# Moving the context chunk's two final states of a bidirectional scan from the mixer stage to the norm behind the output projection

## The chip, the cores and the metric

One core of one Trainium2 chip runs the whole program. The metric is the device time of one execution in microseconds, as a median of several runs. The engines are PE (TensorE matmul; PEld is its weight load), DVE (VectorE), ACT (ScalarE), POOL (GpSimd) and SP (SyncE, which here only issues transfers). Each runs its own instructions in order, and semaphores order them among each other.

## The reference

The kernel is one inference step of a trunk of two layers (model width 1024) over 256 latent tokens and 128 context tokens. Each layer has three token mixers side by side (pooling, differential attention, a bidirectional Mamba-2 scan), a gated merge, an output projection, and a gated FFN with a small convolution. What the change touches is the scan:

```python
def ssd_chunked_scan(x, dt, a, bm, cm, h0):
    ...
    xdt = (x.astype(jnp.float32) * dt[..., None]).reshape(b, nc, q, h, pdim)
    ...
    decay_to_end = jnp.exp(a_cs[..., -1:] - a_cs)
    chunk_states = jnp.einsum('bclhn,bhcl,bclhp->bchpn', bc, decay_to_end, xdt)
    chunk_decay = jnp.exp(a_cs[..., -1])

    def step(state, inp):
        st, dec = inp
        return state * dec[..., None, None] + st, state

    h_final, h_enter = lax.scan(step, h0.astype(jnp.float32), ...)
    ...
    y_off = jnp.einsum('bclhn,bchpn,bhcl->bclhp', cc, h_enter, jnp.exp(a_cs))
    return (y_diag + y_off).reshape(b, n, h, pdim), h_final
```

A chunk has 128 tokens. The 256 latent tokens are chunks 0 and 1, the context is chunk 2. Latent scans start from a given state, so each direction needs one chunk state to enter the other latent chunk. The context scan starts from zero and has a single chunk, so its two chunk states (forward and backward) enter nothing: they are the final states `new_state_ssd`, an output of each layer.

## The kernel before

Every weight tile of 128x128 is split into a high part `wh` and a low part `wl` (ACT rounds, DVE subtracts), and every activation tile likewise (`hh` and `hl`, `mh` and `ml`, `ah` and `al`). A product of the projections is three matmuls (lines 976 to 978). The program is a fixed list of 140 units a layer, each one block of weights of 512 KB at most: XBC 8, U 4, Q 4, K 4, V 4, Z 4, GATE 24, BRANCH 12, OUT 8, UP 44, DOWN 24. Each engine's program is a loop over this list. In unit u ACT and DVE also prepare the weights of unit u + 3, in three buffers (`ahead`; lines 1336 and 1747). All orders are written out by hand in the four engine programs.

From the first Z unit on (MIX0 = unit 24) each unit is also a slot s = u - MIX0 of the mixers. At the end of each slot PE runs a piece of attention or scan between two units, and ACT and DVE have the matching pieces. What matters here:

- Slots 14 to 16, `chunk`: the scan's inputs are transposed into `xt` and `bg`, one chunk each.
- Slots 17 to 20, `chunk_state` (PE, line 1202): one task of `S_TASKS` each, (chunk, direction). DVE weights `xt` into the single buffer `xw` one slot earlier (`weighted`, line 2033), PE makes two fp32 products of 256 columns into `mix7`. Tasks 0 and 1 are the latent ones, and DVE turns them into entering states `hst` (`enter_state`). Tasks 2 and 3 are the context's. ACT copies them from `mix7` into `th` and `cv` (line 1611), and POOL sends these to HBM (line 788).
- Slots 18 and 19: the attention norm. ACT makes the reciprocal roots `rst` (lines 1602 and 1603), DVE applies them to `ot` (line 2124), behind `weighted` of slot 19 and the small `exponents` in its queue.
- From slot 19 on, every second slot, one of six scan tasks y: PE spreads decays over the partitions (`rows`, line 1218), DVE makes exponents (`decays`, line 2058), ACT takes their exp (lines 1621 and 1623), DVE finishes the matrices `ee` (`matrices`, lines 2068 to 2072), and two slots after its `rows` PE reads out (`scan_out`, line 1246). DVE gates the result (`gate_z`, lines 2084 and 2088), which for the first task waits until the state transfers have read `cv`.
- Slot 27 is the last GATE unit; behind it the pooling result `ut` is split into `hh` and `hl` (line 1752), and its memory is free. BRANCH follows (BRANCH0 = unit 52), then OUT (unit 64).

At the norm behind OUT, ahead of the first UP unit (UP0 = unit 72), PE sums squares (`mean_squares`), ACT takes the inverse root and makes the first `hh` (line 1452). Meanwhile PE runs `fill_gap`: three products of 384 columns that nobody reads (line 844). Then `joint` runs the first three UP units tile by tile (line 1075). In UP, ACT reads each bank into `cv` (`evac`, line 1499), DVE adds the convolution's side taps (line 1928), and after each odd unit ACT and DVE split the gated product into `ah` and `al` (lines 1361 and 1752). The tile of index 14 of `al` begins where `ut` lay.

Of the kernel before, what the change touches and what calls it, by code (L numbers as in the profile page):

```python
# [30 lines left out]
P = 128  # L31
# [11 lines left out]
NCH = 3  # L43
# [185 lines left out]
S_TASKS = ((0, 0), (1, 1), (2, 0), (2, 1))  # L229
# [91 lines left out]
def build(nc, wstream, whead, par, bias, tab, xs, xp, cvec, cvec_rows, kc, vc, st0, fng, y, newk, newv, news):  # L321
    ctx = ExitStack()
    with ctx:
# [34 lines left out]
        with ExitStack() as a:  # L358

            head = sb("head", [P, MOD_HEAD, P * KT], where=a)  # L360
# [86 lines left out]
        end_state = [b[:, :, :].rearrange("p a t -> p (a t)")[:, 0:4 * P] for b in (th, cv)]  # L447
# [114 lines left out]
        st_done = sem("st_done")  # L562
        bc_done = sem("bc_done")
# [118 lines left out]
        def _(pool):  # L682
# [68 lines left out]

            pool.wait_ge(head_done, KT // 2)
            pool.dma_start(fg[:, :], fng).then_inc(fg_in, 16)
            for l in range(DEPTH):
# [6 lines left out]
                for u in range(NU):  # L761
                    if u == OUT0:

                        pool.wait_ge(mod_used, sum(lu < (l, OUT0) for lu in MODS))
                        pool.wait_ge(st_out, 32 * (l + 1))
                        pool.wait_ge(gb_done, count(l, 24, 23))
                        pool.dma_start(crow[:, :, :], cvec_rows).then_inc(crow_in, 16)
# [17 lines left out]
                    if u in (MIX0 + SLOT_S + 2, MIX0 + SLOT_S + 3):  # L785
                        k = u - MIX0 - SLOT_S - 2
                        pool.wait_ge(st_done, count(l, 4, 2 + k))
                        pool.dma_start(news[l, k], end_state[k]).then_inc(st_out, 16)
# [34 lines left out]
        def _(pe):  # L823
# [370 lines left out]
            def chunk_state(l, k):  # L1194
                c, d = S_TASKS[k]
                pe.wait_ge(xw_done, count(l, 4, k))
                if k:
                    pe.wait_ge(st_done, count(l, 4, k - 1))
                else:
                    pe.wait_ge(at_done, count(l, NATT, NATT - 1))  # L1200
                for g in range(2):
                    last = mm(mix7[:, 2 * P * g:2 * P * g + 2 * P], bg[:, c, P * g:P * g + P],
                              xw[:, 2 * P * g:2 * P * g + 2 * P], start=True, stop=True)
                last.then_inc(cst_done, 1)

# [16 lines left out]
            def scan_out(l, y_):  # L1222
                c, g = divmod(y_, 2)
                pe.wait_ge(m_done, count(l, NY, y_))
                if y_:
                    pe.wait_ge(yz_done, count(l, NY, y_ - 1))
                else:
                    pe.wait_ge(st_done, count(l, 4, 3))
                    pe.wait_ge(state_in, 32 * (l + 1))
                def term(i, n):  # L1230

                    h = 4 * g + i
                    hs = slice(SSD_P * h, SSD_P * h + SSD_P)
                    ms = slice(P * i, P * i + P)
                    if n == 0:
                        return xt[:, c, hs], ee[:, 0, ms]
                    d = n - 1
                    return hst[:, (0, 3)[d] if c == 0 else (2, 1)[d], hs], eb[:, d, ms]

                nt = 3 if c < 2 else 1  # L1240
                for i0 in (0, 2):
                    for n in range(nt):
                        for i in (i0, i0 + 1):
                            out = mix7[64 * (i % 2):64 * (i % 2) + 64, P * (i // 2):P * (i // 2) + P]
                            s_, m_ = term(i, n)
                            last = mm(out, s_, m_, start=(n == 0), stop=(n == nt - 1))  # L1246
                last.then_inc(y_done, 1)

            def mixers(l, s):
# [26 lines left out]
                if SLOT_S <= s < SLOT_S + 4:  # L1276
                    chunk_state(l, s - SLOT_S)
# [20 lines left out]
            for l in range(DEPTH):  # L1298
# [3 lines left out]
                for u in range(NU):  # L1302
                    if u in (0, UP0):
                        if u:
                            mean_squares(l, M_N2)
                            fill_gap()
# [10 lines left out]
        def _(act):  # L1317
# [233 lines left out]
            def mixers(l, s):  # L1551
# [52 lines left out]
                if SLOT_S + 2 <= s < SLOT_S + 4:  # L1604
                    k = s - SLOT_S
                    act.wait_ge(cst_done, count(l, 4, k))

                    act.wait_ge(bd_done, count(l, 4, 3))

                    act.wait_ge(z_done, count(l, 4, 3))  # L1610
                    af(end_state[k - 2], mix7[:, :], ACT.Copy).then_inc(st_done, 1)
# [38 lines left out]
            for l in range(DEPTH):  # L1650
# [10 lines left out]
                for u in range(NU):  # L1661
# [5 lines left out]
                    if u == PREP and l + 1 < DEPTH:  # L1667
                        params(l + 1)
                    if UNITS[u] in ((OUT, 4, 0), (DOWN, 4, 2)):

                        act.preload_act_table_set(LN_EXP)
# [20 lines left out]
                    for g in done:  # L1692
# [17 lines left out]
                        if kind == BRANCH and j >= 2 * KT:  # L1710
                            high(l, F_MG + j - 2 * KT, mh[:, j - 2 * KT, :], cv[:, j % 2, :])
# [17 lines left out]
        def _(dve):  # L1729
# [293 lines left out]
            def weighted(l, k):  # L2023
# [3 lines left out]
                if k:  # L2027
                    dve.wait_ge(cst_done, count(l, 4, k - 1))
# [7 lines left out]
            def enter_state(l, k):  # L2036

                c, d = S_TASKS[k]
                dve.wait_ge(cst_done, count(l, 4, k))
# [35 lines left out]
            def gate_z(l, y_):  # L2075
# [3 lines left out]
                if y_ == 0:  # L2079

                    dve.wait_ge(st_out, 32 * (l + 1))
# [10 lines left out]
            def mixers_a(l, s):  # L2092
# [25 lines left out]
                if SLOT_S - 1 <= s < SLOT_S + 3:  # L2118
# [90 lines left out]
            for l in range(DEPTH):  # L2209
# [38 lines left out]
                for u in range(NU):  # L2248
# [30 lines left out]
                    for g in done:  # L2279
                        kind, j = GROUPS[g]  # L2280
                        if kind in (XBC, UP):
                            conv_result(l, g)
                            if kind == UP and j % 2:
                                low(l, SP_FF + j // 2, al[:, j // 2, :], cv[:, 1, :], ah[:, j // 2, :])
# [164 lines left out]
```

## Time and profile before

| | |
|---|---|
| median of 3 runs | 1317.59 us (1316.68 to 1317.87) |
| profiled execution | 1317.98 us |
| its span on the core | 1316.2 us |
| PE busy | 1296.3 us (98%) |
| PEld busy | 1243.4 us (94%) |
| DVE busy | 1085.5 us (82%) |
| ACT busy | 652.9 us (50%) |
| POOL busy | 165.9 us (13%) |
| DMA | 210.01 MB, mean 160 GB/s |

The span is the time between the first and the last recorded instruction, and about 1.8 us of the execution lie around it. Busy shares are means over stages that differ, and ends of matmuls are modelled. Idle time of an engine counts only where a later engine waits for it, so waits and timelines have to be read for each stage. Scan and first layer's UP lie at about 255 to 317 us and from 392 us on. The second layer's follow about 637 us later.

### The profile page before, as it was taken

Reading aid. Unit: us, or ns where it says so; the run is one execution under the profiler, and the core shown is the slowest. Engines: PE = TensorE matmul, PEld = TensorE weight load, DVE = VectorE, ACT = ScalarE, POOL = GpSimd, SP = SyncE. Lnnn points to the kernel's source line nnn. Section 1 sums busy time; section 2 is a strip of 40 time slices with the busy share of each in tenths; the row PEclk is TensorE's granted clock in tenths of the full one; section 3 lists DMA queues with packets and bytes.
Section 4 is the critical chain, followed back from the end, with each engine's and each line's share of the span. In section 5 each row is a group of like instructions: output and inputs, shape, how many; then the busy total and the mean of one; then the engine's idle time right before and its main releaser. Section 6 shows DMA issues by size and latency. Waiting matters only on the chain.

```text
span 1316.2 us, 20276 instructions
## 1 busy us (share of the span) xinstructions
PE 1296.3 (98%) x7652; PEld 1243.4 (94%) x7652; DVE 1085.5 (82%) x2038; ACT 652.9 (50%) x1060; POOL 165.9 (13%) x158
## 2 busy tenths in 40 slices
PE   7999999999999999999999999999999999999997
PEld 5999889999999999999999988899999999999997
DVE  6899888688887999999968998878888899999533
ACT  5643545644566454543365335546455744444331
POOL 0077000001220000000103910000032000000010
PEclk9999999999999999999999999999999999999999
DMA  9566345333443354557735552553235243534431
GB/s 363 195 224 224 129 138 200 123 117 113 135 170 112 133 172 133 171 178 264 238 107 192 200 203 78 193 192 111 94 117 192 97 156 133 170 134 164 137 131 50
DMA packets 58641, 210.01 MB, mean 160 GB/s; under 512 B 6704, under 2 KB 9136, under 8 KB 57008
## 3 DMA queue, kind: packets, MB, share of 16 engines
q1 hardware_dynamic: 56512, 199.71, 44.2%
q0 software_dynamic: 2032, 9.00, 2.0%
q8 instruction: 61, 1.00, 0.3%
q14 instruction: 36, 0.29, 0.1%
HBM read 205.02 MB, written 3.67 MB: 159 GB/s over the span
## 4 chain that ended last, share of the span: by engine, by line
PE 77%; DVE 12%; ACT 6%; issue 3%; DMA 1%; SPq 1%; DVEq 0%; ACTq 0%; POOLq 0%
PE acc L976 23%; PE acc L977 22%; PE acc L978 22%; DVE wl L1747 2%; DVE cv L1928 2%; DVE junk_late L1836 1%; PE mix L1246 1%; PE mix L1145 1%; DMA head<-in_whead_dram 1%; DVE gates L1972 1%; ACT th L1372 1%; ACT hh L1361 1%; PE mix L1173 1%; PE mix L1218 1%; ACT wh L1336 1%
## 5 line engine op out<-in xcount | busy, mean ns | idle before, releaser
L976 PE MATMUL acc<-hh,wh 128*128 128x384 f32 x1519 | 517.1, 340 | 0.7 <-DVE wl L1747 0.4
L978 PE MATMUL acc<-hh,wl 128*128 128x384 f32 x1519 | 508.1, 334 | 0.0
L977 PE MATMUL acc<-hl,wh 128*128 128x384 f32 x1519 | 507.9, 334 | 0.0
L1747 DVE TENSOR_TENSOR wl<-raw,wh 128x1024 fp32r<-128x1024 f32 (+1 forms) x276 | 340.9, 1236 | 70.1 <-ACT wh L1336 69.0
L1336 ACT ACTIVATE wh<-raw 128x1024 fp32r<-128x1024 f32 (+1 forms) x276 | 286.9, 1041 | 130.7 <-PE acc L978 128.2
L976 PEld LDWEIGHTS acc<-hh,wh 128*128 128x128 f32 x1519 | 285.2, 188 | 10.3 <-issue 2.9
L977 PEld LDWEIGHTS acc<-hl,wh 128*128 128x128 f32 x1519 | 285.3, 188 | 2.8
L978 PEld LDWEIGHTS acc<-hh,wl 128*128 128x128 f32 x1519 | 285.1, 188 | 0.0
L1928 DVE SCALAR_TENSOR_TENSOR cv<-acc,prm,cv 128x1 f32<-128x1 f32 (+1 forms) x416 | 153.7, 411 | 9.0 <-ACT cv L1499 1.9
L978 PE MATMUL acc<-ah,wl 128*128 128x384 f32 x352 | 117.6, 334 | 0.0
L977 PE MATMUL acc<-al,wh 128*128 128x384 f32 x352 | 117.6, 334 | 0.0
L976 PE MATMUL acc<-ah,wh 128*128 128x384 f32 x352 | 117.6, 334 | 0.0
L1361 ACT ACTIVATE ah<-cv 128x384 fp32r<-128x384 f32 x44 | 23.1, 526 | 132.9 <-DVE cv L1949 132.9
L1836 DVE SCALAR_TENSOR_TENSOR junk_ffn<-rawm,crow 128x1024 f32<-128x1024 f32 x64 | 78.5, 1263 | 0.0
L1836 DVE SCALAR_TENSOR_TENSOR junk_front<-rawm,crow 128x1024 f32<-128x1024 f32 x56 | 74.5, 1365 | 0.0
L1499 ACT ACTIVATE cv<-acc,prm 128x384 f32<-128x384 f32 x104 | 68.3, 656 | 2.4 <-PE acc L978 1.7
L1525 ACT ACTIVATE gates<-acc,bgh 128x384 f32<-128x384 f32 x48 | 27.9, 581 | 78.9 <-PE acc L978 78.9
L976 PEld LDWEIGHTS acc<-ah,wh 128*128 128x128 f32 x352 | 66.1, 188 | 0.0
L977 PEld LDWEIGHTS acc<-al,wh 128*128 128x128 f32 x352 | 66.1, 188 | 0.0
L978 PEld LDWEIGHTS acc<-ah,wl 128*128 128x128 f32 x352 | 66.1, 188 | 0.0
L1537 ACT ACTIVATE th<-cv 128x384 f32<-128x384 f32 x60 | 31.6, 526 | 66.6 <-DVE cv L1928 66.6
L1752 DVE TENSOR_TENSOR al<-cv,ah 128x384 fp32r<-128x384 f32 x44 | 24.6, 559 | 26.0 <-ACT ah L1361 26.0
(310 smaller groups left out, 1704.7 us busy)
## 6 DMA issues: line engine op xcount, KB each, us to landing
raw<-in_wstream_dram SPq DMA_DIRECT2D x248, 512.0 KB, 3.5
rawm<-in_wstream_dram SPq DMA_DIRECT2D x80, 512.0 KB, 4.2
raw<-in_wstream_dram SPq DMA_DIRECT2D x32, 448.0 KB, 3.3
head<-in_whead_dram SPq DMA_DIRECT2D x8, 1024.0 KB, 15.2
crow_late<-in_cvec_rows_dram POOLq DMA_DIRECT2D x2, 1024.0 KB, 6.7
crow<-in_cvec_rows_dram POOLq DMA_DIRECT2D x2, 1024.0 KB, 5.3
out_y_dram<-yt SPq DMA_DIRECT2D x3, 384.0 KB, 2.3
x<-in_xs_dram SPq DMA_DIRECT2D x1, 1024.0 KB, 8.6
```

The costliest lines, as they stand in the source:

```text
L976: mm(out, sh, mhi, start=start, stop=False)
L977: mm(out, sh, mlo, start=False, stop=False)
L978: return mm(out, sl, mhi, start=False, stop=stop)
L1336: af(wh[:, s, 0:n], raw[:, raw_slot(u), 0:n], ACT.Copy).then_inc(hi_done, 1)
L1361: af(dst, src, ACT.Copy).then_inc(h_hi, 1)
L1499: af(cv[:, b_, :], bank[:, 0:T], ACT.Identity, bias=prm_(b, tile), scale=prm_(w, 3 * tile + 1)) \
L1525: af(gates[:, j, :], bank[:, 0:T], ACT.Tanh, bias=bgh[:, j:j + 1], scale=0.5).then_inc(g_done, 1)
L1537: af(th[:, b_, :], cv[:, b_, :], ACT.Tanh).then_inc(cv_tanh, 1)
L1747: tt(wl[:, s, 0:n], raw[:, raw_slot(u), 0:n], wh[:, s, 0:n].bitcast(F32), ALU.subtract).then_inc(lo_done, 1)
L1752: tt(dst, src, high_.bitcast(F32), ALU.subtract).then_inc(h_lo, 1)
L1836: last = stt(out=junk[:, v, :], in0=rawm[:, n % NMOD, :], scalar=1.0, in1=rows[:, v, :], op0=ALU.mult, op1=ALU.mult, accum_out=macc[:, m, ...
L1928: return stt(out=out, in0=src, scalar=prm_(w, 3 * tile + i), in1=out, op0=ALU.mult, op1=ALU.add)
```

## The change

`S_TASKS` keeps the two latent tasks. The context's two chunk states leave slots 19 and 20, with them DVE's `weighted` for them (slots 18 and 19), ACT's two copies, and the transfers from `th` and `cv`. The waits of DVE's `gate_z` and of POOL (ahead of OUT) on the state transfers go too.

In their place POOL, at its place in front of the first BRANCH unit, copies the context's `bg` into a new tile `bge` and multiplies the context's `xt` with the two directions' weights into `xwe` (`end_factors`). Both tiles lie where `ut` lay, and POOL waits for DVE's last split of `ut`. PE makes the four products of 256 columns at the norm behind OUT, into `mix6` and `mix7`, in place of `fill_gap` (which stays at the start of layer 2). ACT copies the two banks back into `xwe` at unit 4 of UP, ahead of that unit's `evac`, and POOL sends them at unit 6. ACT waits for `end_factors` before it writes `mh` over `xt`, and DVE waits for the transfers before it writes `al` of index 14, in unit 29 of UP.

```diff
-S_TASKS = ((0, 0), (1, 1), (2, 0), (2, 1))
+S_TASKS = ((0, 0), (1, 1))
+ENDS_COPY, ENDS_OUT = UP0 + 4, UP0 + 6
+ENDS_FREE = 14
...
+            sb("under_ends", [P, 36 * T], where=a)
+            bge = sb("bge", [P, 2 * P], where=a)
+            xwe = sb("xwe", [P, 2, 4 * P], where=a)
...
+            def end_factors(l):
+
+                pool.wait_ge(h_lo, count(l, NSPLIT, SP_OP + 3))
+                pool.wait_ge(xt_in, count(l, NCH, 2))
+                pool.wait_ge(wdc_done, l + 1)
+                nc.gpsimd.tensor_copy(bge[:, :], bg[:, 2, 0:2 * P]).then_inc(xwe_done, 1)
+                for d in range(2):
+                    at = (NCH * d + 2) * SSD_H
+                    nc.gpsimd.tensor_tensor(xwe[:, d, :].rearrange("p (h q) -> p h q", h=SSD_H),
+                                            xt[:, 2, :].rearrange("p (h q) -> p h q", h=SSD_H),
+                                            wdc[:, at:at + SSD_H].unsqueeze(2).to_broadcast([P, SSD_H, SSD_P]),
+                                            ALU.mult).then_inc(xwe_done, 1)
...
                     if u == OUT0:
...
-                        pool.wait_ge(st_out, 32 * (l + 1))
...
-                    if u in (MIX0 + SLOT_S + 2, MIX0 + SLOT_S + 3):
-                        k = u - MIX0 - SLOT_S - 2
-                        pool.wait_ge(st_done, count(l, 4, 2 + k))
-                        pool.dma_start(news[l, k], end_state[k]).then_inc(st_out, 16)
+                    if u == BRANCH0:
+                        end_factors(l)
+                    if u == ENDS_OUT:
+                        for d in range(2):
+                            pool.wait_ge(ends_kept, count(l, 2, d))
+                            pool.dma_start(news[l, d], xwe[:, d, :]).then_inc(st_out, 16)
...
+            def end_states(l):
+
+                pe.wait_ge(xwe_done, 3 * (l + 1))
+                for d, bank in enumerate((mix6, mix7)):
+                    for g in range(2):
+                        last = mm(bank[:, 2 * P * g:2 * P * g + 2 * P], bge[:, P * g:P * g + P],
+                                  xwe[:, d, 2 * P * g:2 * P * g + 2 * P], start=True, stop=True)
+                    last.then_inc(ends_done, 1)
...
-                if SLOT_S <= s < SLOT_S + 4:
+                if SLOT_S <= s < SLOT_S + 2:
                     chunk_state(l, s - SLOT_S)
...
                             mean_squares(l, M_N2)
-                            fill_gap()
+                            end_states(l)
...
-                if SLOT_S + 2 <= s < SLOT_S + 4:
-                    k = s - SLOT_S
-                    act.wait_ge(cst_done, count(l, 4, k))
-
-                    act.wait_ge(bd_done, count(l, 4, 3))
-
-                    act.wait_ge(z_done, count(l, 4, 3))
-                    af(end_state[k - 2], mix7[:, :], ACT.Copy).then_inc(st_done, 1)
...
+                    if u == ENDS_COPY:
+                        for d, bank in enumerate((mix6, mix7)):
+                            act.wait_ge(ends_done, count(l, 2, d))
+                            af(xwe[:, d, :], bank[:, :], ACT.Copy).then_inc(ends_kept, 1)
...
                         if kind == BRANCH and j >= 2 * KT:
+                            if j == 2 * KT:
+                                act.wait_ge(xwe_done, 3 * (l + 1))
...
-                if y_ == 0:
-
-                    dve.wait_ge(st_out, 32 * (l + 1))
...
-                if SLOT_S - 1 <= s < SLOT_S + 3:
+                if SLOT_S - 1 <= s < SLOT_S + 1:
                     weighted(l, s - SLOT_S + 1)
...
                             if kind == UP and j % 2:
+                                if j // 2 == ENDS_FREE:
+                                    dve.wait_ge(st_out, 32 * (l + 1))
                                 low(l, SP_FF + j // 2, al[:, j // 2, :], cv[:, 1, :], ah[:, j // 2, :])
```

The counts of `xw_done`, `st_done` and `cst_done` follow from the shorter list (2 in place of 4).

## Rows read from the trace of the kernel before

**Rows 1.** Windows of the scan stage: us, busy of PE, PEld, DVE, ACT, POOL, then clock.
```profile
232.00:345.00 113.00, 113.00 (x700) 107.26 (x699) 89.99 (x175) 60.94 (x87) 12.73 (x10) 1.00 0.33 113
297.40:315.90 18.50, 18.50 (x113) 17.73 (x110) 18.18 (x44) 8.81 (x13) 0.00 (x0) 1.00 0.24 78
```

**Rows 2.** Waits of the whole trace: total us, times, longest.
```profile
PEld acc L976 <- DVE wl L1747: 2.3, 7, 0.7
...
PEld mix L1246 <- DVE ee L2072: 0.5, 2, 0.3
...
DVE cv L2084 <- DMA out_news_dram<-cv: 3.7, 2, 1.8
```

**Rows 3.** Timeline of PE, first layer: start us, us, instruction.
```profile
254.17 1.03 PE L1202 MATMUL mix<-xw,bg 128*128 128x256 f32 x4
254.85 0.81 PE L1218 MATMUL mix<-bd,selr 96*128 96x512 f32 x2
...
259.69 1.03 PE L1202 MATMUL mix<-xw,bg 128*128 128x256 f32 x4
...
260.73 0.34 PE L977 MATMUL acc<-hl,wh 128*128 128x384 f32 x1
```

**Rows 4.** Timeline of PEld, first layer; idle time and its end in brackets.
```profile
264.81 0.21 PEld L1246 LDWEIGHTS mix<-ee,xt 128*64 128x64 f32 x4 [0.25 <-DVE ee L2072]
...
316.24 0.42 PEld L1246 LDWEIGHTS mix<-ee,xt 128*64 128x64 f32 x8 [0.25 <-issue]
```

**Rows 5.** Timeline of DVE, first layer, from slot 18's end to the first scan.
```profile
255.31 0.69 DVE L2033 TENSOR_TENSOR xw<-xt,wdc 128x512 f32<-128x512 f32 x1 [1.94 <-PE mix L1202]
...
256.22 2.21 DVE L2124 SCALAR_TENSOR_TENSOR ot<-ot,sg,rst 128x384 f32<-128x384 f32 x4
...
263.83 0.69 DVE L2072 TENSOR_TENSOR ee<-ee,bg 128x512 f32<-128x512 f32 x1
```

**Rows 6.** Timeline of ACT, first layer, the last step of the attention norm.
```profile
253.81 1.49 ACT L1603 ACTIVATE rst<-rst 128x1536 f32<-128x1536 f32 x1
```

**Rows 7.** Timeline of PE across the gap before the first UP unit.
```profile
389.61 2.10 PE L844 MATMUL mix<-tb 128*128 128x384 f32 x6
391.92 0.41 PE L1075 MATMUL acc<-hh,wh 128*128 128x384 f32 x1 [0.21 <-ACT hh L1452]
```

**Rows 8.** Timeline of ACT: the slot before unit 4 of UP, and two 512-wide reads.
```profile
260.79 1.09 ACT L1621 ACTIVATE eb<-mix 128x512 f32<-128x512 f32 x2 [2.16 <-DVE ee L2058]
...
417.92 0.53 ACT L1361 ACTIVATE ah<-cv 128x384 fp32r<-128x384 f32 x1 [2.30 <-DVE cv L1949]
418.35 0.66 ACT L1499 ACTIVATE cv<-acc,prm 128x384 f32<-128x384 f32 x1
```

**Rows 9.** Timeline of DVE at units 3 and 4 of UP.
```profile
419.10 1.51 DVE L1928 SCALAR_TENSOR_TENSOR cv<-acc,prm,cv 128x1 f32<-128x1 f32 x4
420.54 1.22 DVE L1747 TENSOR_TENSOR wl<-raw,wh 128x1024 fp32r<-128x1024 f32 x1
```

**Rows 10.** Timeline of PEld at units 7 and 11 of UP.
```profile
421.81 0.19 PEld L976 LDWEIGHTS acc<-hh,wh 128*128 128x128 f32 x1 [0.22 <-DVE wl L1747]
...
438.79 0.19 PEld L976 LDWEIGHTS acc<-hh,wh 128*128 128x128 f32 x1 [0.38 <-DVE wl L1747]
```

**Rows 11.** Timeline of DVE from the split of ut to the last scan.
```profile
297.32 1.96 DVE L1752 TENSOR_TENSOR hl<-ut,hh 128x384 fp32r<-128x384 f32 x4 [1.71 <-ACT hh L1361]
...
299.96 0.49 DVE L2088 SCALAR_TENSOR_TENSOR zz<-cv,zz 128x128 f32<-128x128 f32 x2
...
315.22 0.69 DVE L2072 TENSOR_TENSOR ee<-ee,bg 128x512 f32<-128x512 f32 x1
```

**Rows 12.** Timeline of POOL: its first work after the scan, and one sum.
```profile
321.76 3.00 POOL L793 TENSOR_TENSOR gates<-gates 128x384 f32<-128x384 f32 x2 [56.20 <-DVE gates L1972]
...
376.77 1.64 POOL L696 TENSOR_TENSOR sqa<-sqa,th 128x384 f32<-128x384 f32 x1 [1.42 <-ACT th L1481]
```

**Rows 13.** Timeline of DVE beside that sum.
```profile
377.45 2.04 DVE L1836 SCALAR_TENSOR_TENSOR junk_late<-rawm,crow 128x1024 f32<-128x1024 f32 x1
```

More of the change, by code:

```diff
@@ L228 @@
 M_DT, M_DTT, M_SM, M_PW, M_ATT, M_SSD, M_N2 = 1, 2, 3, 4, 8, 12, 14
-S_TASKS = ((0, 0), (1, 1), (2, 0), (2, 1))
+S_TASKS = ((0, 0), (1, 1))
+ENDS_COPY, ENDS_OUT = UP0 + 4, UP0 + 6
+ENDS_FREE = 14
+assert FT * T + ENDS_FREE * T == 36 * T
 ROTATE_SLOTS = (0, 1, 2, 3, 5, 6)
@@ L358, in build @@
         with ExitStack() as a:
+            sb("under_ends", [P, 36 * T], where=a)
+            bge = sb("bge", [P, 2 * P], where=a)
+            xwe = sb("xwe", [P, 2, 4 * P], where=a)
+        with ExitStack() as a:
             head = sb("head", [P, MOD_HEAD, P * KT], where=a)
@@ L445, in build @@
         dtc = gates[:, 13, :]
-        end_state = [b[:, :, :].rearrange("p a t -> p (a t)")[:, 0:4 * P] for b in (th, cv)]
         head_bank = [(mix7, mix5)[p % 2][:, 8 * (p // 2):8 * (p // 2) + 8] for p in range(KT // 2)]
@@ L562, in build @@
         st_done = sem("st_done")
+        xwe_done = sem("xwe_done")
+        ends_done = sem("ends_done")
+        ends_kept = sem("ends_kept")
         bc_done = sem("bc_done")
@@ L1195, in chunk_state @@
                 c, d = S_TASKS[k]
-                pe.wait_ge(xw_done, count(l, 4, k))
+                pe.wait_ge(xw_done, count(l, 2, k))
                 if k:
-                    pe.wait_ge(st_done, count(l, 4, k - 1))
+                    pe.wait_ge(st_done, count(l, 2, k - 1))
                 else:
@@ L1227, in scan_out @@
                 else:
-                    pe.wait_ge(st_done, count(l, 4, 3))
+                    pe.wait_ge(st_done, count(l, 2, 1))
                     pe.wait_ge(state_in, 32 * (l + 1))
@@ L2027, in weighted @@
                 if k:
-                    dve.wait_ge(cst_done, count(l, 4, k - 1))
+                    dve.wait_ge(cst_done, count(l, 2, k - 1))
                 else:
@@ L2038, in enter_state @@
                 c, d = S_TASKS[k]
-                dve.wait_ge(cst_done, count(l, 4, k))
+                dve.wait_ge(cst_done, count(l, 2, k))
                 dve.wait_ge(state_in, 32 * (l + 1))
```

## The prediction

> **What bounds the kernel now.** I read the page's busy shares first, then the stage table, then the tensor engine's waits, and last the timelines of the places that the change touches. The stage table says who sets the pace of the scan: over 113.00 us PE is busy for all 113.00 at full clock, while DVE is busy for 89.99 and ACT for 60.94 [rows 1]. So a product taken out of this stage should bring the end nearer, unless something else is as late as the product. The waits show where that is so. PE's weight loads wait for the low weight halves of DVE seven times, 2.3 us in all, and twice (once a layer) for DVE's scan matrix `ee`, 0.5 us [rows 2]. Both places matter here: the first scan readout, and the first units of UP. The matrices' 0.25 us is no loss: the last readout shows the same 0.25 us with nothing named as its cause [rows 4]. But it says that DVE's matrix and PE arrive together there.
>
> Both layers run the same program, so I work on layer 1's rows and double.
>
> **Part 1: two products fewer a layer in the scan (PE).** Chunk states 2 and 3, four fp32 products of 256 columns, go. State 2 holds up the next product from 254.17 to 254.85, 0.68 us. State 3 starts at 259.69 and the second product behind it at 260.73, 1.04 us; without it that product stands two steps of 0.17 us behind, so 0.87 us are its own [rows 3]. PE reaches the first readout 0.68 + 0.87 = 1.55 us earlier, at 264.81 - 1.55 = 263.26.
>
> It can't start then, for `scan_out(0)` waits for DVE's matrix, which was ready at 263.83 + 0.69 = 264.52 [rows 5]. What moves that? DVE loses two weightings (`xw`) and ACT two copies; ACT had been idle 2.16 us before its exponentials of this slot, waiting for DVE [rows 8], so only DVE's part could count. DVE's chain is: third `xw` at 255.31, attention norm at 256.22, exponents, weight half, matrices. Without the `xw` and with the small `exponents` done early, the norm starts when ACT's `rst` is ready: 253.81 + 1.49 = 255.30, say 255.35 [rows 5, 6]. That ACT chain lies ahead of the removed work and doesn't move. DVE gains 256.22 - 255.35 = 0.87 us, and the matrix is ready at 263.65. If the 0.25 us in front of the readout's load runs beside the wait, the load starts at 263.70 (gain 1.11); if it follows, at 263.95 (gain 0.86). I take **1.0 us a layer**, bounds 0.86 and 1.11, or 1.55 if this wait isn't real. After this readout PE is the later one again: the wait of DVE on the state DMA (3.7 us in two) disappears as well [rows 2], so DVE has more room in the next slots. That wait is worth nothing by itself, since PE stood nowhere for it.
>
> **Part 2: the products at the norm (PE).** Three products of 384 columns (1152 columns) give way to four of 256 (1024). The old ones start at 389.61 and last 2.10 us, and PE then waits 0.21 us for ACT's `hh` before 391.92 [rows 7]. By columns the new ones last about 1.9 us, so `hh` still ends the gap: cost 0, and if all the products showed in full it would still be below nothing by 0.2. `xwe_done` is some 85 us old by then.
>
> **Part 3: two copies on ACT at unit 4 of UP.** ACT's queue is in order. Before, it makes `ah` at 417.92 and reads the next bank into `cv` at 418.35; DVE's taps follow at 419.10, the low half of the weights at 420.54 to 421.76, and PE, which stands waiting, loads at 421.81 [rows 8 to 10]. The copies come exactly between `ah` and that read. Two 512-wide reads of PSUM took 1.09 us together [rows 8]; less the 0.1 us by which neighbours overlap (417.92 + 0.53 against 418.35) they push the read back by 1.0. ACT's 2.30 us of idle lie ahead of `ah`, not behind it, so they don't hide it. DVE's `al` (0.56 us) ended just ahead of the taps. So taps, `wl` and PE's unit 7 all come **1.0 us** later. Is it made good? At unit 11 PE waits for `wl` again, 0.38 us [rows 10], so DVE is still the later one 17 us on, and both are late by the same. Cost 1.0 a layer; bounds 0 (DVE catches up) and 1.2 (both copies without overlap).
>
> The DMAs go out on POOL's queue behind unit 6, where POOL has nothing else to do until the squares of DOWN; DVE's wait for them is at unit 29, 23 units later, and four units take 438.79 - 421.81 = 17.0 us [rows 10]. Nothing is queued behind it in time: 0.
>
> **Part 4: the operands put aside by POOL.** POOL has been idle since the scan's DMAs and stays so for 56.20 us [rows 12], so `end_factors` starts as soon as DVE has written the four low parts of `ut`: 297.32 + 1.96 = 299.28 [rows 11]. That is one copy of 256 columns and two multiplications of 512. The nearest row is 1.64 us for 384 columns [rows 12], so at most 0.7 + 2.2 + 2.2, at least 0.5 + 1.3 + 1.3: POOL is at work until about 302.4 to 304.4. What is beside it? DVE, without a pause: 18.18 us of the 18.50 between 297.40 and 315.90 [rows 1], with the last matrix ready at 315.22 + 0.69 = 315.91 and PE's last readout loading at 316.24 after its 0.25 us, that is, from 315.99 on [rows 4, 11]. DVE has 0.1 to 0.3 us of slack here. And POOL does slow DVE: a product of two SBUF operands beside POOL's sum took 2.04 us [rows 13], where most such instructions of its size take 1.22, as the weight half does [rows 9]. It ended 1.08 us after POOL's sum did (376.77 + 1.64 = 378.41). The two gating instructions at 299.96 read two SBUF operands, and the weight half behind the decays does too; the decays read PSUM. I take one and a half such hits, 1.2 us, less 0.2 of slack: **1.0 us a layer**. Bounds: 0, if POOL falls wholly beside the decays; 3.0, if the gating pair is held for both multiplications.
>
> The Trainium skill, SBUF — State Buffer, section "Who interferes with whom", says that DVE with two SBUF inputs and GpSimd reading SBUF exclude each other for a whole instruction. The row agrees: 378.41 and nearly one full 1.22 us more make 2.04. By that rule DVE's gating pair can be held for whole multiplications, which is the third rival below.
>
> **Sum.** A layer: - 1.0 (part 1) + 0 + 1.0 (part 3) + 1.0 (part 4) = + 1.0. Two layers: + 2.0. The profiled execution took 1317.98 us (span 1316.2); that gives 1320.0. It lies 0.4 above the median of the runs, 1317.59, so the predicted median is **1319.6 us**. 0.2% of it, 2.6 us, is about what can be told from no change.
>
> **The rivals.**
>
> *POOL's work is hidden.* It falls beside the decays, which read PSUM, or its instructions are short. For it: DVE's eight decays fill 2.1 of the 4 us. Against it: the gating pair stands right in front of them. Parts 1 and 3 then cancel: + 0.0, 1317.6.
>
> *PE's products are all that counts.* Neither the first readout nor unit 7 waits for DVE, as the full PE rows of rows 1 suggest. Then 2 x 1.55 = 3.1 us come off, and nothing of parts 3 and 4 shows: 1314.5, faster. It decides if DVE's matrix comes by 263.26 and DVE has 1.0 us at unit 7. Against it: 264.52 and the wait at 421.81.
>
> *POOL holds DVE longer.* The gating pair is held by both multiplications: 3.0 less 0.2 of slack, 2.8 a layer. 2 x (- 1.0 + 1.0 + 2.8) = + 5.6: 1323.2, slower.
>
> **How the numbers follow.** Forecast 0.42, hidden 0.26, products alone 0.10, longer hold 0.22. Range 1315.2 to 1323.2: it leaves out most of the faster rival and the upper half of the longer hold. The forecast's own range is 1318.2 to 1321.2, and some 0.12 of its 0.42 lie above + 2.6. Faster 0.10; slower 0.12 + 0.22 = 0.34; the same 0.56.
>
> **What would show it.** Part 1: PE idle about 0.55 us, or up to 0.3 more, before the first readout, which starts about 1.0 us earlier than 264.8, waiting for DVE `ee`. Part 2: the first product of UP still released by ACT `hh`. Part 3: at unit 7 PE waits 1.2 us for `wl`, not 0.22, in each layer. Part 4: DVE's gating pair or weight half longer beside POOL, and PE waiting about 1 us for `ee` at the last readout. The prediction is wrong if the last readout doesn't wait, or if the wait at unit 7 is shorter than 1 us.

## The result, and the profile after

The changed kernel takes 1320.13 us in the median of nine runs (1319.86 to 1322.84), the kernel before beside it 1317.26 us (1316.42 to 1317.87, nine runs). The ratio is 1.0024, with a 95% interval of 1.0015 to 1.0033. That is 2.87 us more between the medians. The interval lies above 1, so the kernel is slower, by about 0.2%. The profiled spans are 1318.1 and 1316.2 us, 1.9 apart.

The busy times show that the work did leave PE: 1292.8 us after, 1296.3 before, 3.5 less. The time went up all the same, so it went into waits. The waits of the whole trace after (engine and line, what it waited for: total us, times, longest) name them:

```profile
PEld mix L1278 <- DVE ee L2102: 5.5, 6, 1.4
PEld acc L999 <- DVE wl L1777: 4.2, 7, 1.2
```

The readout (L1278, before L1246) waits for the scan matrix six times where it waited twice, 5.5 us in place of 0.5, and the low weight halves cost 4.2 in place of 2.3 [rows 2]. To see what each wait cost, I follow the same weight load of PE through both traces. First the loads of the kernel before that are not among the rows above, on the timeline of PEld (start us, us, instruction, idle time before it and what ended it):

```profile
211.64 0.30 PEld L1145 LDWEIGHTS mix<-kt,qt 64*128 64x128 f32 x4 [0.17 <-issue]
...
417.47 0.19 PEld L976 LDWEIGHTS acc<-hh,wh 128*128 128x128 f32 x1 [0.22 <-DVE wl L1747]
...
776.50 0.30 PEld L1145 LDWEIGHTS mix<-kt,qt 64*128 64x128 f32 x4 [0.25 <-issue]
...
902.31 0.21 PEld L1246 LDWEIGHTS mix<-ee,xt 128*64 128x64 f32 x4 [0.25 <-DVE ee L2072]
...
944.17 0.42 PEld L1246 LDWEIGHTS mix<-ee,xt 128*64 128x64 f32 x8 [0.25 <-issue]
...
953.74 0.42 PEld L1246 LDWEIGHTS mix<-ee,xt 128*64 128x64 f32 x8 [0.25 <-issue]
...
1054.90 0.19 PEld L976 LDWEIGHTS acc<-hh,wh 128*128 128x128 f32 x1 [0.22 <-DVE wl L1747]
...
1059.24 0.19 PEld L976 LDWEIGHTS acc<-hh,wh 128*128 128x128 f32 x1 [0.22 <-DVE wl L1747]
```

And the same places of the kernel after, same view:

```profile
210.55 0.30 PEld L1168 LDWEIGHTS mix<-kt,qt 64*128 64x128 f32 x4 [0.17 <-issue]
...
262.67 0.20 PEld L1278 LDWEIGHTS mix<-ee,xt 128*64 128x64 f32 x4 [0.95 <-DVE ee L2102]
...
304.53 0.42 PEld L1278 LDWEIGHTS mix<-ee,xt 128*64 128x64 f32 x8 [0.30 <-DVE ee L2102]
...
315.24 0.42 PEld L1278 LDWEIGHTS mix<-ee,xt 128*64 128x64 f32 x8 [1.35 <-DVE ee L2102]
...
320.34 0.30 PEld L1318 LDWEIGHTS misc<-rst,tb 128*128 128x128 f32 x2 [0.40 <-issue]
...
416.73 0.19 PEld L999 LDWEIGHTS acc<-hh,wh 128*128 128x128 f32 x1 [0.23 <-DVE wl L1777]
...
422.04 0.19 PEld L999 LDWEIGHTS acc<-hh,wh 128*128 128x128 f32 x1 [1.18 <-DVE wl L1777]
...
776.73 0.30 PEld L1168 LDWEIGHTS mix<-kt,qt 64*128 64x128 f32 x4 [0.25 <-issue]
...
901.50 0.20 PEld L1278 LDWEIGHTS mix<-ee,xt 128*64 128x64 f32 x4 [0.95 <-DVE ee L2102]
...
943.64 0.42 PEld L1278 LDWEIGHTS mix<-ee,xt 128*64 128x64 f32 x8 [0.58 <-DVE ee L2102]
...
954.35 0.42 PEld L1278 LDWEIGHTS mix<-ee,xt 128*64 128x64 f32 x8 [1.36 <-DVE ee L2102]
...
1055.85 0.19 PEld L999 LDWEIGHTS acc<-hh,wh 128*128 128x128 f32 x1 [0.21 <-DVE wl L1777]
...
1061.16 0.19 PEld L999 LDWEIGHTS acc<-hh,wh 128*128 128x128 f32 x1 [1.18 <-DVE wl L1777]
```

Each difference, less the difference at the station before, is what the stretch between them cost:

| station | layer 1: after - before | step | layer 2: after - before | step |
|---|---|---|---|---|
| first attention product in the layer's mixers | 210.55 - 211.64 = -1.09 | | 776.73 - 776.50 = +0.23 | |
| first readout | 262.67 - 264.81 = -2.14 | -1.05 | 901.50 - 902.31 = -0.81 | -1.04 |
| fifth readout | 304.53 - 306.67 = -2.14 | 0 | 943.64 - 944.17 = -0.53 | +0.28 |
| last readout | 315.24 - 316.24 = -1.00 | +1.14 | 954.35 - 953.74 = +0.61 | +1.14 |
| unit 6 of UP | 416.73 - 417.47 = -0.74 | +0.26 | 1055.85 - 1054.90 = +0.95 | +0.34 |
| unit 7 of UP | 422.04 - 421.81 = +0.23 | +0.97 | 1061.16 - 1059.24 = +1.92 | +0.97 |
| sum | | +1.32 | | +1.69 |

A station is one and the same weight load of PE in both programs. The readouts before that are not in the lines above are those of [rows 4] and 306.67, and unit 7 before is in [rows 10].

The -1.09 of the first station lies ahead of every changed instruction of layer 1: it is a difference between the two profiled executions, not of the change. The kernel before with another order in slot 18 (before_norm_early, below) runs the same code up to there and has this load at 210.59, like the kernel after. 1.32 + 1.69 = 3.01 us are the change's, and 3.01 - 1.09 = 1.92 is the 1.9 between the spans. The medians, 2.87 apart, agree with the 3.01.

**At the first readout** PE stands idle for 0.95 us. DVE's queue shows why, and then what happened at the last readout (timeline of DVE after):

```profile
254.31 1.15 DVE L2151 SCALAR_TENSOR_TENSOR ot<-ot,sg,rst 128x384 f32<-128x384 f32 x2 [2.46 <-ACT rst L1635]
...
261.92 0.69 DVE L2102 TENSOR_TENSOR ee<-ee,bg 128x512 f32<-128x512 f32 x1
...
297.81 0.95 DVE L2115 SCALAR_TENSOR_TENSOR zz<-cv,zz 128x128 f32<-128x128 f32 x1
299.73 2.15 DVE L2088 SCALAR_TENSOR_TENSOR ee<-mix,nac,tb 128x128 f32<-128x128 f32 x8
```

The attention norm now starts as soon as ACT's `rst` is there, with 2.46 us of idle ahead of it, and the matrix is ready at 261.92 + 0.69 = 262.61, just before PE's load at 262.67. The idle time there is 0.95 us and was 0.25 [rows 4], 0.70 more, and the load came 1.05 earlier, so PE itself arrived 1.05 + 0.70 = 1.75 us earlier and got 1.05 of it. Counted from the station, the matrix came 0.82 us earlier (262.61 - 210.55 = 52.06, before 264.52 - 211.64 = 52.88), and the other 0.23 is that the load now follows it by 0.06 us and not by 0.29.

**Ahead of the last readout** the gating pair takes 2.00 us where it took 0.49 [rows 11]. Beside it, on the timeline of POOL after (the first multiplication, then both together):

```profile
297.20 0.40 POOL L766 COPY bge<-bg 128x256 f32<-128x256 f32 x1 [75.23 <-DVE hl L1782]
297.57 1.03 POOL L769 TENSOR_TENSOR xwe<-xt,wdc 128x512 f32<-128x512 f32 x1
297.57 2.09 POOL L769 TENSOR_TENSOR xwe<-xt,wdc 128x512 f32<-128x512 f32 x2
```

and on that of DVE, the second of the pair:

```profile
298.68 1.13 DVE L2115 SCALAR_TENSOR_TENSOR zz<-cv,zz 128x128 f32<-128x128 f32 x1
```

The first of DVE's two small instructions ends at 297.81 + 0.95 = 298.76, which is 0.16 us after POOL's first multiplication (297.57 + 1.03 = 298.60). The second ends at 298.68 + 1.13 = 299.81, 0.15 us after POOL's second (297.57 + 2.09 = 299.66). So each of the pair is held through one multiplication. The eight decays right behind take 2.15 us as ever. The last readout then waits 1.35 us. Of these, 1.35 - 0.25 = 1.10 are new, which agrees with the step of 1.14.

**Ahead of layer 2's fifth readout** there is a second delay. Timelines of ACT (both layers) and of DVE (layer 2) after:

```profile
301.97 1.06 ACT L1647 ACTIVATE ee<-ee 128x1024 f32<-128x1024 f32 x1 [4.64 <-DVE ee L2088]
...
941.08 1.06 ACT L1647 ACTIVATE ee<-ee 128x1024 f32<-128x1024 f32 x1 [4.92 <-DVE ee L2088]
```
```profile
942.17 0.69 DVE L2100 TENSOR_TENSOR ee<-ee 128x512 f32<-128x512 f32 x1 [0.34 <-ACT ee L1647]
```

In layer 1 ACT takes the exponential 0.09 us after DVE's last decay (299.73 + 2.15 = 301.88). In layer 2 it takes it 0.38 us after (938.55 + 2.15 = 940.70), and DVE stands idle 0.34 us for it. The traces of all eight kernels with the change have this late start in layer 2 (0.37 or 0.38 us), with POOL beside the pair or not; the two kernels without it (before and before_norm_early) have 0.10 and 0.09 us there. With the pair held, this is the step of 0.28 us. Why ACT starts late is not shown.

**Behind the last readout** a second, smaller wait appears. The sum of squares in slot 32 (L1318), which had no idle time before, has 0.40 us at 320.34. The timeline of ACT shows what it waits for, and further on the edit at unit 4 of UP:

```profile
319.38 0.85 ACT L1652 ACTIVATE rst<-zz 128x768 f32<-128x768 f32 x1 [3.75 <-DVE zz L2115]
...
417.18 0.53 ACT L1393 ACTIVATE ah<-cv 128x384 fp32r<-128x384 f32 x1 [2.30 <-DVE cv L1979]
417.61 1.07 ACT L1696 ACTIVATE xwe<-mix 128x512 f32<-128x512 f32 x2
418.56 0.67 ACT L1531 ACTIVATE cv<-acc,prm 128x384 f32<-128x384 f32 x1
```

ACT's squares wait 3.75 us for DVE's last gating `zz`, before the change 2.6, because DVE's queue is still late. At 417.61 the two copies stand between `ah` and the read of the next bank, which goes to 418.56 where it would have followed at about 417.61. DVE's taps wait for it, and then PE's unit 7, 1.18 us in place of 0.22 [rows 10] (timeline of DVE after):

```profile
419.34 0.74 DVE L1958 SCALAR_TENSOR_TENSOR cv<-acc,prm,cv 128x1 f32<-128x1 f32 x2 [1.05 <-ACT cv L1531]
```

Last the products at the norm, on the timeline of PE after, which answers to [rows 7]:

```profile
388.88 1.89 PE L1234 MATMUL mix<-xwe,bge 128*128 128x256 f32 x8
...
391.19 0.41 PE L1098 MATMUL acc<-hh,wh 128*128 128x384 f32 x1 [0.42 <-ACT hh L1484]
```

They take 1.89 us in place of 2.10, and ACT's `hh` still ends the gap, now of 0.42 us. From the first of these products to the first of UP it is 391.19 - 388.88 = 2.31 us, and before 391.92 - 389.61 = 2.31: the place costs nothing.

### The profile page after: what moved, and what is told of

Read it like the earlier page. It is cut to its first block, busy times and chain, and to the rows that moved or that the text cites. A ratio compares the mean times of both kernels' runs of the same rounds, so it can differ in the third digit from the quotient of the medians.

```text
span 1318.1 us, 20246 instructions
## 1 busy us (share of the span) xinstructions
PE 1292.8 (98%) x7640; PEld 1240.3 (94%) x7640; DVE 1085.6 (82%) x2034; ACT 652.2 (49%) x1060; POOL 170.9 (13%) x164
## 4 chain that ended last, share of the span: by engine, by line
PE 75%; DVE 13%; ACT 6%; issue 3%; DMA 1%; SPq 1%; DVEq 0%; ACTq 0%
PE acc L999 23%; PE acc L1000 22%; PE acc L1001 22%; DVE cv L1958 2%; DVE wl L1777 2%; DMA head<-in_whead_dram 1%; DVE gates L2002 1%; PE mix L1168 1%; DVE ee L2088 1%; ACT th L1404 1%; ACT hh L1393 1%; PE mix L1196 1%; PE mix L1278 1%; DVE hl L1782 1%; PE misc L1298 1%
```

## The experiments

All are built on the changed kernel but one. Nothing is left out of the computation in any of them. The ratios are against the kernel before, measured beside them with a median of 1316.97 us over 30 runs, in each of two sets. The changed kernel has only its own median of 1320.13 from the first measurement, so comparisons with it are between medians of two measurements. The kernel before itself differs by 1317.26 - 1316.97 = 0.29 us between them.

### The copies in ACT's idle time (copies_in_idle)

```diff
-                    if u == ENDS_COPY:
-                        for d, bank in enumerate((mix6, mix7)):
-                            act.wait_ge(ends_done, count(l, 2, d))
-                            af(xwe[:, d, :], bank[:, :], ACT.Copy).then_inc(ends_kept, 1)
...
                             conv_silu(l, g)
+                            if u == ENDS_COPY + 1:
+                                for d, bank in enumerate((mix6, mix7)):
+                                    act.wait_ge(ends_done, count(l, 2, d))
+                                    af(xwe[:, d, :], bank[:, :], ACT.Copy).then_inc(ends_kept, 1)
                             if kind == UP and j % 2:
```

> The changed kernel with ScalarE's two copies of the final states made at unit 5 of UP, directly before ah, where ScalarE stood idle 2.6 us waiting for VectorE, and not at unit 4 between ah and the next bank's read. Theory A (the copies cost because they stand between ah and the read that VectorE waits for): the wait at unit 7 of UP goes back from 1.18 to 0.22 us in both layers, so 2 x 0.97 = 1.9 us less than the changed kernel, about 1.0 us above the kernel before. Theory B (ScalarE's extra work costs wherever it stands, or the delay is made good before the next wait for the weights): the time stays that of the changed kernel, 2.9 above before.

Measured: 1318.31 us (1317.59 to 1319.92), ratio 1.0009 [1.0001, 1.0018]. Timelines of PEld and of ACT in this kernel:

```profile
421.28 0.19 PEld L999 LDWEIGHTS acc<-hh,wh 128*128 128x128 f32 x1 [0.20 <-DVE wl L1777]
```
```profile
422.06 1.07 ACT L1723 ACTIVATE xwe<-mix 128x512 f32<-128x512 f32 x2
424.76 0.53 ACT L1393 ACTIVATE ah<-cv 128x384 fp32r<-128x384 f32 x1 [1.62 <-DVE cv L1979]
```

The copies take their 1.07 us as before, and `ah` behind them still has 1.62 us of idle. The wait at unit 7 is 0.20 us again. 1320.13 - 1318.31 = 1.8 us came back for 2 x 0.97 in the ledger. Part 3 cost what its place cost, and not what the copies cost.

### POOL's work behind the scan (pool_after_scan)

```diff
                 pool.wait_ge(wdc_done, l + 1)
+                pool.wait_ge(yz_done, count(l, NY, NY - 1))
                 nc.gpsimd.tensor_copy(bge[:, :], bg[:, 2, 0:2 * P]).then_inc(xwe_done, 1)
```

> The changed kernel with GpSimd's copy and two multiplications begun only when VectorE has gated the last scan result (3 semaphore waits became 4). Theory A (GpSimd holds up VectorE's gating pair, VectorE has no slack up to the last readout): the pair goes back from 2.0 to 0.49 us, the 1.35 us idle before the last readout to 0.25, and the idle before the scan's sums to nothing; 1.4 us in layer 1 and 1.8 in layer 2 come back, 3.2 us in all, so slightly below the kernel before (- 0.3). Theory B (the last readout waits for another reason, such as the removed transfer wait having moved the work): the wait at the last readout stays above 1 us and the time stays.

Measured: 1317.20 us (1316.84 to 1317.47), ratio 1.0002 [0.9993, 1.0011]: 2.9 us below the changed kernel, where the ledger has 1.40 + 1.76 = 3.16 for this part. Timeline of PEld at layer 1's last readout, and at layer 2's sum of squares:

```profile
314.33 0.42 PEld L1279 LDWEIGHTS mix<-ee,xt 128*64 128x64 f32 x8 [0.25 <-issue]
...
956.72 0.30 PEld L1319 LDWEIGHTS misc<-rst,tb 128*128 128x128 f32 x2 [0.34 <-issue]
```

The last readout is back at 0.25 us. Of the small wait at slot 32, layer 1 keeps nothing and layer 2 keeps 0.34 us, though POOL holds nothing ahead of it any more. What the layers differ in is ACT's late exponential: DVE waits 0.34 us for it in this kernel too, in layer 2 only. With PE's products gone, PE arrives where DVE is, and this delay shows.

### Both moved (both_moved)

Both edits above.

> Both moves together. Theory A: the two delays add up and nothing else was displaced, so what is left is the gain at the first readout, 1.05 us a layer: 2.1 us below the kernel before, 1315.2. Theory B (one delay hides behind the other): less than 1 us below before.

Measured: 1315.32 us (1314.94 to 1316.36), ratio 0.9987 [0.9978, 0.9996]. The two costs add: 1.8 + 2.9 = 4.7, and 1320.13 - 1315.32 = 4.8. What is left of the change is part 1, a gain of 1316.97 - 1315.32 = 1.65 us, where the ledger has 2 x 1.05; the wait at layer 2's sum of squares (0.32 us here) takes most of the difference. At layer 2's fifth readout the idle time is back at 0.25 us with no releaser, though ACT's exponential is as late as in the changed kernel: without POOL's hold DVE has room for it. So that step of 0.28 needed both.

### Two dead products in the scan (probe_products)

Two fp32 products of 256 columns stand in slot 20 again, where chunk state 3 stood; nothing reads them, and DVE's and ACT's work stays away.

```diff
+                if s == SLOT_S + 3:
+                    pe.wait_ge(st_done, count(l, 2, 1))
+                    for g in range(2):
+                        mm(mix7[:, 2 * P * g:2 * P * g + 2 * P], bg[:, 1, P * g:P * g + P],
+                           xw[:, 2 * P * g:2 * P * g + 2 * P], start=True, stop=True)
```

> The changed kernel with two fp32 products of 256 columns that nobody reads put back into slot 20 of each layer, where the context's fourth state was; nothing is computed for them by VectorE, and nothing reads them. Theory A (the first readout waits for VectorE's matrix, not for the products): 0.87 us of product work a layer meet 0.70 us of idle time, so each layer grows by about 0.2 us and the time by 0.3. Theory B (product time counts in full): 2 x 0.87 = 1.7 us more than the changed kernel.

Measured: 1320.38 us (1320.19 to 1321.68), ratio 1.0027 [1.0016, 1.0037], 0.25 above the changed kernel. Timeline of PEld in this kernel:

```profile
211.04 0.30 PEld L1168 LDWEIGHTS mix<-kt,qt 64*128 64x128 f32 x4 [0.17 <-issue]
...
263.34 0.20 PEld L1278 LDWEIGHTS mix<-ee,xt 128*64 128x64 f32 x4 [0.25 <-DVE ee L2107]
```

Counted from the attention station, the readout comes at 263.34 - 211.04 = 52.30 us, against 262.67 - 210.55 = 52.12 after the change. Products that take PE about 0.87 us cost 0.18, and the idle time falls from 0.95 to 0.25 us. They fill a wait. That "PE's products are all that counts" is refuted: behind the change DVE's matrix sets this readout, and 0.7 of those 0.87 us are time in which PE would only wait.

### POOL beside the decays (beside_decays)

Is it any DVE instruction that POOL holds up, or only some? Here the copies are moved as in the first experiment, and POOL starts when the gating pair is done, so that its multiplications lie beside the eight decays.

```diff
+                pool.wait_ge(yz_done, count(l, NY, 3))
```

> As both_moved, but GpSimd's copy and multiplications begin when VectorE has gated the fourth scan result (task 3), so that their 2.5 us fall beside the eight decays, each of which reads one operand from PSUM, and no longer beside the gating pair, which reads two from SBUF. Against the changed kernel GpSimd starts only about 1.3 us later. Theory A (only instructions with two SBUF operands are held): decays stay at 2.15 us, the weight half behind them is held by at most 0.4 us, and the last readout waits at most 0.1 us more than in both_moved: 1315.3. Theory B (any VectorE work beside GpSimd is slowed): the decays grow by over 1 us and most of the 3 us of copies_in_idle against both_moved stays: about 1318.

Measured: 1315.40 us (1315.19 to 1316.12), ratio 0.9988 [0.9979, 0.9997], the same as with POOL behind the scan. Timelines of DVE and of POOL in this kernel:

```profile
298.66 0.49 DVE L2116 SCALAR_TENSOR_TENSOR zz<-cv,zz 128x128 f32<-128x128 f32 x2
299.07 2.15 DVE L2089 SCALAR_TENSOR_TENSOR ee<-mix,nac,tb 128x128 f32<-128x128 f32 x8
301.14 1.68 DVE L1778 TENSOR_TENSOR wl<-raw,wh 128x1024 fp32r<-128x1024 f32 x1
```
```profile
299.69 2.04 POOL L770 TENSOR_TENSOR xwe<-xt,wdc 128x512 f32<-128x512 f32 x2
```

The pair is at 0.49 us. The decays, which read one operand from PSUM and one from SBUF, lie beside POOL's multiplications from 299.69 on and take 2.15 us as without them. The weight half behind them, two SBUF operands, starts at 301.14, before POOL ends at 299.69 + 2.04 = 301.73, and takes 1.68 us in place of 1.22. Which instruction is beside POOL decides, not how much of DVE's time is. The Trainium skill, SBUF — State Buffer, section "Who interferes with whom", has this as a DVE instruction with two SBUF inputs contending with a GpSimd instruction that reads SBUF, under an exclusive lock. The rows agree: the weight half, with two SBUF inputs, grew from 1.22 to 1.68 us, and the decays, with one, kept their 2.15.

### The attention norm early (both_norm_early)

With both costs moved away, the first readout still waits. DVE's norm stands behind ACT's `rst`. In ACT's queue of slot 18 the gate bank's evacuation comes first, which waits 3.77 us for PE, and the rounding of the next weights, the table load (1.28 us) and the logarithm of `dte` follow, all ahead of `rst`. Here ACT loads the table and takes the logarithm first, in that idle time, and evacuates the gate bank behind the norm. The rest is as in both_moved.

```diff
-                    if h == HEADS - 1:
-                        act.preload_act_table_set(LN_EXP)
-                        act.wait_ge(dt_floor, l + 1)
-                        af(dte[:, :], dte[:, :], ACT.Ln).then_inc(ln_done, 1)
...
+                    if u == MIX0 + SLOT_A + HEADS - 1:
+                        act.preload_act_table_set(LN_EXP)
+                        act.wait_ge(dt_floor, l + 1)
+                        af(dte[:, :], dte[:, :], ACT.Ln).then_inc(ln_done, 1)
                     for g in done:
-                        if GROUPS[g][0] in (XBC, UU, QQ, KK, VV, ZZ, GATE, UP):
+                        if GROUPS[g][0] in (XBC, UU, QQ, KK, VV, ZZ, GATE, UP) and u != MIX0 + SLOT_A + HEADS - 1:
                             evac(l, g)
...
                         mixers(l, s)
+                        if s == SLOT_A + HEADS - 1:
+                            evac(l, done[0])
```

> As both_moved, and in slot 18 ScalarE loads the table of the logarithm and takes the logarithm of the time steps while it waits for the gate product, and evacuates that gate product only behind the attention norm. That takes about 2.0 us (0.58 gate, 1.28 table, 0.24 logarithm) off the way to rst. Theory A (the first readout waits for the chain rst, norm, decays, matrices): the 0.95 us idle in front of the first readout shrinks to 0.25 in both layers, 2 x 0.70 = 1.4 us less than both_moved: 1313.9. Theory B (something else holds the first readout, or the next limit is as near): no change against both_moved.

Measured: 1313.59 us (1313.39 to 1314.52), ratio 0.9974 [0.9964, 0.9984]. It is the fastest of all, 3.4 us under the kernel before. Timelines of DVE and of PEld in this kernel:

```profile
252.36 1.15 DVE L2154 SCALAR_TENSOR_TENSOR ot<-ot,sg,rst 128x384 f32<-128x384 f32 x2 [0.49 <-ACT rst L1632]
```
```profile
210.57 0.30 PEld L1169 LDWEIGHTS mix<-kt,qt 64*128 64x128 f32 x4 [0.17 <-issue]
...
261.98 0.20 PEld L1279 LDWEIGHTS mix<-ee,xt 128*64 128x64 f32 x4 [0.25 <-issue]
```

DVE's norm starts at 252.36 in place of 254.31, and the first readout no longer waits for DVE: its 0.25 us have no releaser. It comes 261.98 - 210.57 = 51.41 us behind the station; in both_moved it was 262.93 - 210.80 = 52.13. So 0.72 us a layer, 1.4 in all, came from here, of 1315.32 - 1313.59 = 1.7.

### The same early norm in the kernel before (before_norm_early)

The same edit of ACT's order, on the kernel before, without the change.

> The kernel before with the same reordering of ScalarE in slot 18 and nothing else. Theory A (in the kernel before the matrix and the products are ready together, so the products alone set the pace): the first readout starts when it did, the time stays within 0.2 us. Theory B (the chain of VectorE set the pace in the kernel before too): faster by up to 1 us a layer.

Measured: 1317.16 us (1316.71 to 1317.71), ratio 1.0000 [0.9991, 1.0008]. Timelines of DVE and of PEld in this kernel:

```profile
254.25 0.69 DVE L2035 TENSOR_TENSOR xw<-xt,wdc 128x512 f32<-128x512 f32 x1 [1.94 <-PE mix L1202]
```
```profile
210.59 0.30 PEld L1145 LDWEIGHTS mix<-kt,qt 64*128 64x128 f32 x4 [0.17 <-issue]
...
263.75 0.21 PEld L1246 LDWEIGHTS mix<-ee,xt 128*64 128x64 f32 x4 [0.25 <-DVE ee L2074]
```

263.75 - 210.59 = 53.16 us, and in the kernel before 264.81 - 211.64 = 53.17: nothing. The gain exists only behind the change. But here DVE's norm stood behind the third `xw`, which waits 1.94 us for PE's chunk state, so this run could not free DVE's chain. It does not tell whether PE's products or DVE's chain alone set the first readout before the change; the two arrive together there.

### Early norm, POOL beside the decays (decays_norm_early)

beside_decays with the early norm.

> beside_decays with the reordering of slot 18. Theory A: the same 1.4 us as both_norm_early gets, less whatever the weight half held behind the decays costs: 1313.9 to 1314.3. Theory B: no gain on beside_decays.

Measured: 1314.09 us (1313.76 to 1315.33), ratio 0.9978 [0.9969, 0.9987]. It is 0.5 above both_norm_early, and the intervals overlap. The sum of squares has 0.40 us of idle in layer 1, where both_norm_early has none; between last readout and sum lie 318.46 - 313.35 = 5.11 us against 318.14 - 313.36 = 4.78. So some 0.3 of the 0.5 have a place. beside_decays had the same 0.40 us at 320.03 and yet the time of both_moved, so 0.3 us is as far as these medians reach.

## Why the prediction was right, and where a term was off

The forecast was +2.0 us for the profiled execution (1319.6 in the median); measured are +1.9 in the spans and +2.87 in the medians (1320.13). The ledger says why the two differ: 3.01 us of the change, and -1.09 ahead of it in the profiled execution. So the close match of +2.0 and +1.9 is luck. The change itself costs 1.0 us more than forecast: -2.09 for part 1 (forecast -2.0), +1.94 for part 3 (+2.0), and +3.16 for part 4 (+2.0).

- **Part 1, forecast -1.0 a layer: -1.05 and -1.04.** Right in cause and size. The matrix was expected 0.87 us earlier and came 0.82 earlier; the load follows it closely, as the upper bound of 1.11 had it. The idle time of 0.95 lies above the 0.55 to 0.85 forecast, because PE arrives 1.75 us earlier and not 1.55: the 0.68 for state 2 was too low, the dead products, which are state 3's, took 0.88 (0.18 of time and 0.70 of idle), and two of these are 1.76. That DVE is the limit is shown by the dead products, which cost 0.18 of 0.87, and by the early norm, which gives back 0.72.
- **Part 2, forecast 0: 0.** The gap still ends with `hh`.
- **Part 3, forecast +1.0: +0.97 in both layers**, shown by moving the two copies alone, which gives 1.8 us back.
- **Part 4, forecast +1.0: +1.40 and +1.76.** The term that was mis-sized. The cause, POOL holding DVE ahead of the last readout, is shown by two kernels that give it back (1.0002, and with the copies 0.9987 or 0.9988). The step that failed is "I take one and a half such hits, 1.2 us". The pair was held through both multiplications, one for each of its instructions, which is what the rival "POOL holds DVE longer" said. But POOL's three instructions took 0.40 + 2.09 = 2.5 us, under my lower estimate of 3.1, so the hold was 2.00 - 0.49 = 1.51 us, not 3.0. At the last matrix 1.41 of it are left: it is ready at 314.49 + 0.69 = 315.18, and would have been at 315.91 - 2.14 = 313.77, since PE's fifth readout comes 2.14 us earlier. 0.27 us of slack, within the 0.1 to 0.3 forecast, leave the 1.14 of the last readout. The two errors, a longer hold and shorter work, nearly cancelled there, which is luck too. What I missed is what is late next: the squares of slot 32 (0.26 and 0.34), and in layer 2 the fifth readout (0.28), where ACT's late exponential comes on top. DVE had 18.18 of 18.50 us busy [rows 1], so nothing let it catch up behind the last readout either.
- **The rivals.** "POOL's work is hidden" fell with the 2.00 us pair, and came true once POOL was put beside the decays. "Products alone" fell with the dead products. The third had the mechanism and missed the price.

What stays open: why ACT takes the exponential ahead of layer 2's fifth readout about 0.3 us late in every kernel with the change. It is what parts layer 2's fifth readout (0.58 us of idle) from layer 1's (0.30), and it precedes the 0.34 us at slot 32 in layer 2 with POOL out of the way. No run removes it.

## What to carry to other kernels

Work taken from the busiest engine is worth only the distance to the next one that is late: here 1.75 us of products gave 1.05, and the rest came (0.72) when the engine behind was let go earlier. What is moved to idle engines is priced by its place in their order: the same 1.07 us of copies cost 0.97 at one spot of ACT's queue and nothing one unit on, and the same 2 us of POOL cost 1.1 to 1.8 beside DVE's two-SBUF-operand instructions and next to nothing beside its PSUM reads. After each stall that you price, follow the late engine to its next two consumers; in a stage where it is 98% busy they are late as well.

## What the hardware showed that I had not expected

- A pair of DVE instructions of 0.49 us took 2.00 beside two POOL multiplications issued back to back. Its first instruction ended 0.16 us after the first multiplication and its second 0.15 us after the second: one at a time, and each short instruction was held until the multiplication beside it had ended.
- POOL's multiplication of 128x512 with a broadcast operand took 1.03 or 1.04 us (2.04 and 2.09 for two), while its sum of 128x384 had taken 1.64 [rows 12]. The estimate by columns from that row was too high by a factor of two. A wait inside the 1.64 explains it, and the trace of the kernel before shows it on DVE's timeline:

```profile
376.31 1.23 DVE L1747 TENSOR_TENSOR wl<-raw,wh 128x1024 fp32r<-128x1024 f32 x1 [0.67 <-ACT wh L1336]
```

DVE's weight half, with two SBUF operands, ran until 377.54. POOL's sum, recorded from 376.77, ended 0.87 us after that. The sum at 373.98 took 1.37 us, and ended 0.87 us after a weight half too (373.26 + 1.22 = 374.48). So 0.87 us is about the sum's own time, and by columns from there (an estimate) a multiplication takes 1.16. POOL's copy of 128x256 shows the same: it took 0.40 us beside a DVE instruction that reads PSUM, and 1.23 in pool_after_scan (from 318.30), where DVE's weight half ran from 318.05 to 319.27. So DVE holds POOL up too, and a POOL row taken beside DVE is no price for a free POOL.
